# Four transformer blocks on one core: each norm joined to the stage before it, and one stage in place of load, first modulation and first norm

## What is computed

```python
def modulate(x, shift, scale):
    return layer_norm(x) * (1.0 + scale[:, None, :]) + shift[:, None, :]
```

## Time and profile before

| what | before |
|---|---|
| median of 3 runs | 3742.06 us (3732.88 to 3747.66) |
| the profiled execution's own time | 3748.66 us |
| its span, first to last instruction | 3746.9 us |
| mean granted TensorE clock | 0.957 |
| PE busy | 3398.1 us (91%) |
| DVE busy | 2617.8 us (70%) |
| ACT busy | 1756.9 us (47%) |
| DMA | 637.35 MB, mean 170 GB/s |

### The profile page before, as it was taken

How to read it: one execution, slowest core, us unless ns; L and a number is a source line. 1 busy time by engine, 2 the same in 40 slices (tenths; PEclk the granted TensorE clock), 3 DMA queues, 4 the chain that set the end, 5 groups by cost and what they waited for, 6 DMA issues and landing times. The chain is left out here.

```text
span 3746.9 us, 60692 instructions
## 1 busy us (share of the span) xinstructions
PE 3398.1 (91%) x19830; PEld 2989.5 (80%) x19830; DVE 2617.8 (70%) x5085; ACT 1756.9 (47%) x3251; POOL 224.5 (6%) x106
## 2 busy tenths in 40 slices
PE   4989889899999979989799999999968799898798
PEld 3877777789999968878587799999957699687697
DVE  5578669778787875566589687878756466445565
ACT  2353316755555544434239555555533254444353
POOL 0011000001011100100000011101101000001000
PEclk9989999999999989989899999999989899999899
DMA  5327432277777756237231577777741243552243
GB/s 208 122 65 268 164 119 91 92 236 249 256 246 242 250 180 195 64 128 254 79 124 40 189 243 242 249 254 247 241 162 71 79 167 137 173 187 96 91 186 118
DMA packets 256319, 637.35 MB, mean 170 GB/s; under 512 B 39088, under 2 KB 66224, under 8 KB 250000
## 3 DMA queue, kind: packets, MB, share of 16 engines
q1 hardware_dynamic: 217924, 561.56, 45.1%
q10 hardware_dynamic: 38220, 73.55, 5.7%
HBM read 633.89 MB, written 1.15 MB: 169 GB/s over the span
## 5 line engine op out<-in xcount | busy, mean ns | idle before, releaser
L147 PE MATMUL experts_ps_h<-uP_hi,experts_u_hi 128*128 128x256 f32 x1728 | 489.2, 283 | 1.6 <-DVE experts_u_lo L142 1.3
L149 PE MATMUL experts_ps_h<-uP_hi,experts_u_lo 128*128 128x256 f32 x1728 | 489.0, 283 | 0.0
L148 PE MATMUL experts_ps_h<-uP_lo,experts_u_hi 128*128 128x256 f32 x1728 | 488.9, 283 | 0.0
L142 DVE TENSOR_TENSOR experts_u_lo<-kept,experts_u_hi 128x512 fp32r<-128x512 f32 x432 | 354.2, 836 | 147.4 <-ACT experts_u_hi L139 135.6
L139 ACT ACTIVATE experts_u_hi<-kept 128x512 fp32r<-128x512 f32 x432 | 268.6, 630 | 342.3 <-PE experts_ps_h L149 271.1
L142 DVE TENSOR_TENSOR experts_v_lo<-u_w,experts_v_hi 128x512 fp32r<-128x512 f32 x432 | 298.2, 690 | 85.1 <-ACT experts_v_hi L139 77.5
L147 PEld LDWEIGHTS experts_ps_h<-uP_hi,experts_u_hi 128*128 128x128 f32 x1728 | 330.7, 191 | 15.0 <-DVE experts_u_lo L142 6.7
L147 PE MATMUL expert_y<-experts_v_hi,experts_w_hi 128*128 128x512 f32 x864 | 339.1, 392 | 1.1 <-DVE experts_w_lo L142 1.1
L148 PE MATMUL expert_y<-experts_v_lo,experts_w_hi 128*128 128x512 f32 x864 | 338.8, 392 | 0.0
L148 PEld LDWEIGHTS experts_ps_h<-uP_lo,experts_u_hi 128*128 128x128 f32 x1728 | 330.7, 191 | 7.5
L149 PE MATMUL expert_y<-experts_v_hi,experts_w_lo 128*128 128x512 f32 x864 | 336.1, 389 | 0.0
(11 more groups left out here) (547 smaller groups left out, 8105.9 us busy)
## 6 DMA issues: line engine op xcount, KB each, us to landing
u_w<-in_peer_v SPq DMA_DIRECT2D x256, 512.0 KB, 4.4
kept<-in_peer_u SPq DMA_DIRECT2D x216, 512.0 KB, 4.5
kept<-in_ada_w_all ACTq DMA_DIRECT2D x140, 512.0 KB
up_w<-in_ffn_w_up SPq DMA_DIRECT2D x44, 1024.0 KB, 5.5
od_in_w<-in_od_w_in SPq DMA_DIRECT2D x36, 1024.0 KB, 5.1
in_w<-in_w_in SPq DMA_DIRECT2D x48, 752.0 KB, 4.3
turns<-in_w_gate SPq DMA_DIRECT2D x32, 1024.0 KB, 6.4
down_w<-in_ffn_w_down SPq DMA_DIRECT2D x44, 512.0 KB, 3.3
```

The lines of the kernel that those rows point to most:

```text
L142: return dve.tensor_tensor(self.lo[at], value, self.hi[at].bitcast(F32), ALU.subtract)
L147: pe.matmul(out, left.hi[left_at], right.hi[right_at], start=start, stop=False, skip_group_check=skip)
L148: pe.matmul(out, left.hi[left_at], right.lo[right_at], start=False, stop=False, skip_group_check=skip)
L149: return pe.matmul(out, left.lo[left_at], right.hi[right_at], start=False, stop=stop, skip_group_check=skip)
```

## The change

The three first stages become one, `first_norm`. ada_w's columns come in eight transfers of 1 MB, in turn a quarter of the shift columns (512 columns, half of the rows; `wide`) and a quarter of the scale columns (256 columns, 1 KB runs; `slim`). DVE makes the shift half as before, PE the scale half directly: 64 f32 matmuls whose moving operand is one silu column and whose output is a column of scale; no row goes through DRAM. x's statistics and norm run between these. `norm_turn` is taken apart into the class `TurnedNorm`, whose steps are called from the stage before: `turn_project_norm`, `residual_norm_turn` and, for the norm after the first feed-forward, `conv_ffn` itself. Steps go row tile by row tile: ACT makes u of b = 0, DVE that of b = 1 in two halves; PE turns each tile on its own, and DVE and ACT take four chunks of 128 tokens each. Gate and residual are done in halves of 512 columns, as soon as that half of the projection is done; norm, g and b of `Residual` take two passes in place of three. The next stage's weights are issued in the joined stage, with one exception: of the expert choice only the first query weight (0.5 MB) is, while `choose_and_gate` itself now loads the keys (1 MB) and the other three. The third block's feed-forward tiles also hold the first weights of the fourth block's projection, which are loaded once the last of them is split. The seven norm stages that are joined and two of the three first ones end no more with the waits and the clearing of L76 to L78; a joined stage has the semaphores of both of its parts to clear.

```diff
+    def turn(self, pe, b, after_columns=True):
+        if after_columns:
+            pe.wait_ge(self.cols_done, 1)
+        for h in range(2):
+            pe.wait_ge(self.u_done[b], h + 1 if b else 1)
+            for k in range(h * 4, h * 4 + 4):
+                mm = pe.transpose(self.ps[:, b, k], self.u[:, b, k * P:(k + 1) * P], self.g.ident[:])
+            mm.then_inc(self.turned, 1)
...
+    def first_rows(self, act):
+        act.wait_ge(self.rstd_done, 1)
+        act.activation(self.u[:, 0], self.x[:, 0], ACT.Identity, bias=0.0 if self.rms else self.minus[:],
+                       scale=self.rstd[:, 0]).then_inc(self.u_done[0], 1)
...
+    def second_rows(self, dve, link):
+        dve.wait_ge(self.root_done, 2)
+        link(dve.reciprocal(self.rstd[:, 1], self.sd[:, 1]))
+        for h in range(2):
+            at = slice(h * 512, (h + 1) * 512)
...
+            else:
+                ins = dve.tensor_scalar(self.u[:, 1, at], self.x[:, 1, at], self.mv[:, 1, 0:1], self.rstd[:, 1],
+                                        ALU.subtract, ALU.mult)
+            ins.then_inc(self.u_done[1], 1)
...
+    def half_on_vector(self, dve, b):
+        dve.wait_ge(self.turned, 2 * b + 1)
+        for k in range(0, 4):
+            ins = dve.tensor_scalar(self.uT[:, k, b * P:(b + 1) * P], self.ps[:, b, k], self.scale[:, k:k + 1], self.cols[:, k:k + 1],
+                                    ALU.mult, ALU.add)
+        ins.then_inc(self.uT_vector, 1)
+
+    def half_on_act(self, act, b):
+        act.wait_ge(self.turned, 2 * b + 2)
+        act.wait_ge(self.cols_done, 1)
+        for k in range(4, KD):
+            ins = act.activation(self.uT[:, k, b * P:(b + 1) * P], self.ps[:, b, k], ACT.Identity, bias=self.cols[:, k:k + 1],
+                                 scale=self.scale[:, k:k + 1])
+        ins.then_inc(self.uT_act, 1)
+
...
+    def high(self, act, b):
+        for h, done in enumerate((self.uT_vector, self.uT_act)):
+            act.wait_ge(done, b + 1)
+            at = (slice(None), slice(h * 4, h * 4 + 4), slice(b * P, (b + 1) * P))
+            self.uP.write_hi(act, at, self.uT[at]).then_inc(self.hi_done, 1)
...
+def first_norm(nc, name, g, consts, c_all, x_in, ada_w, ada_b, x, uP, memory, ahead):
+    WIDE, SLIM, HK = 512, 256, KD // 2
+    SLIMS = D // SLIM
...
+                def load_wide(j):
+                    v, h = divmod(j, 2)
+                    at = slice(h * HK, (h + 1) * HK)
+                    sync.dma_start(wide[v][:, at], w[:, at, v * WIDE:(v + 1) * WIDE]).then_inc(wide_in[j], 16)
+
+                sync.dma_start(c16[:, 0], c_all[0]).then_inc(c_in, 16)
+                sync.dma_start(c16[:, 1], c_all[2]).then_inc(c_in, 16)
+                for j in range(SLIMS):
+                    load_wide(j)
+                    sync.dma_start(slim[j], w[:, :, D + j * SLIM:D + (j + 1) * SLIM]).then_inc(slim_in[j], 16)
                 for first in ahead:
                     first(sync)
+                sync.dma_start(g.iota[:], consts[1]).then_inc(iota_in, 16)
+                sync.wait_ge(iota_in, 16)
...
+                def slim_products(j):
+                    pe.wait_ge(slim_in[j], 16)
+                    for c in range(SLIM // P):
+                        at = KD + j * (SLIM // P) + c
+                        for k in range(KD):
+                            mm = pe.matmul(ps_c[:, at:at + 1], slim[j][:, k, c * P:(c + 1) * P], g.silu[:, 0, k:k + 1],
+                                           start=k == 0, stop=k == KD - 1)
+                    return mm
+
+                def wide_sums(v):
+                    pe.wait_ge(acc_done, v + 1)
+                    for c in range(WIDE // P):
+                        at = v * (WIDE // P) + c
+                        mm = pe.matmul(ps_c[:, at:at + 1], acc[:, v, c * P:(c + 1) * P], ones[:], start=True, stop=True)
...
+                slim_products(0)
+                slim_products(1)
+                norm.turn(pe, 0, False)
+                wide_sums(0)
+                slim_products(2)
+                norm.turn(pe, 1, False)
+                slim_products(3)
+                wide_sums(1).then_inc(sums_done, 1)
+                stay_awake(pe, ps_w[:, 0:T], g.ident[:], x[:, 0, 0:T], 7)
...
+                act.dma_start(g.ident[:], consts[0]).then_inc(ident_in, 16)
+                act.dma_start(bias[:], ada_b[0:2 * D].rearrange("(k p) -> k p", p=P)).then_inc(bias_in, 16)
+                act.dma_start(x[:], x_in).then_inc(x_in_done, 16)
...
+                add_up(0)
+                dve.wait_ge(x_in_done, 16)
+                norm.stats(dve, link, 0)
+                add_up(1)
+                norm.stats(dve, link, 1)
+                norm.first_factors(dve, link)
+                add_up(2)
+                norm.second_rows(dve, link)
+                add_up(3)
+                dve.wait_ge(bias_turned, 1)
+                dve.wait_ge(sums_done, 1)
+                link(dve.tensor_copy(norm.cols[:], ps_c[:, 2 * KD:4 * KD]))
+                link(dve.tensor_tensor(norm.cols[:], norm.cols[:], ps_c[:, 0:2 * KD], ALU.add))
+                link(dve.tensor_scalar_add(norm.scale[:], norm.cols[:, KD:2 * KD], 1.0))
...
+    def weigh(self, dve, link, b, h):
+        at = slice(h * 512, (h + 1) * 512)
+        r = self.r[:, b, at]
         dve.wait_ge(self.gate_in, 16)
...
-            link(dve.reciprocal(self.sd[:, b], self.sd[:, b]))
-            link(dve.tensor_scalar(x[:, b], self.r[:, b], self.mv[:, b, 0:1], self.sd[:, b], ALU.subtract, ALU.mult))
-            link(dve.tensor_tensor(x[:, b], x[:, b], self.g[:], ALU.mult))
-            link(dve.tensor_tensor(x[:, b], x[:, b], self.b[:], ALU.add))
+        link(dve.tensor_tensor(r, self.y[:, b, at], self.gate[:, at], ALU.mult))
+        link(dve.scalar_tensor_tensor(out=r, in0=self.x[:, b, at], scalar=DN_ALPHA, in1=r, op0=ALU.mult, op1=ALU.add))
+        link(dve.bn_stats(self.st[:, b, h, :], r))
+
+    def close(self, dve, link, b):
+        link(dve.bn_aggr(self.mv[:, b, :], self.st[:, b].rearrange("p a b -> p (a b)")))
+        dve.tensor_scalar_add(self.sd[:, b], self.mv[:, b, 1:2], LN_EPS).then_inc(self.stats_done, 1)
+
+    def centre(self, dve, link, b):
+        dve.wait_ge(self.rows_in, 32)
+        link(dve.scalar_tensor_tensor(out=self.r[:, b], in0=self.r[:, b], scalar=self.mv[:, b, 0:1], in1=self.g[:],
+                                      op0=ALU.subtract, op1=ALU.mult))
+
+    def finish(self, dve, link, b):
+        dve.wait_ge(self.root_done, b + 1)
+        link(dve.reciprocal(self.sd[:, b], self.sd[:, b]))
+        link(dve.scalar_tensor_tensor(out=self.x[:, b], in0=self.r[:, b], scalar=self.sd[:, b], in1=self.b[:],
+                                      op0=ALU.mult, op1=ALU.add))
...
+def turn_project_norm(nc, name, g, src, pre, x, gate_row, ln_rows, row, gain_cols, uP, uT, ahead, room=None, spare=None):
...
+                norm.load(sync)
+                for first in ahead:
+                    first(sync)
...
+                    if b:
+                        norm.turn_rows(pe)
...
+                        if h:
+                            mm.then_inc(y_done, 1)
+                for b in range(TB):
+                    norm.turn(pe, b)
+                stay_awake(pe, y[:, 0, 0:T], g.ident[:], x[:, 0, 0:T], 7)
...
+                if ln_rows:
+                    res.root(act, 0)
+                norm.root(act, 0)
+                norm.first_rows(act)
+                if ln_rows:
+                    res.root(act, 1)
+                norm.half_on_act(act, 0)
+                norm.root(act, 1)
+                norm.high(act, 0)
+                norm.half_on_act(act, 1)
+                norm.high(act, 1)
...
+                for h in range(2):
+                    weigh(0, h)
+                if ln_rows:
+                    res.close(dve, link, 0)
+                    res.centre(dve, link, 0)
+                    res.finish(dve, link, 0)
+                norm.stats(dve, link, 0)
+                norm.columns(dve, link)
+                norm.first_factors(dve, link)
+                for h in range(2):
+                    weigh(1, h)
+                if ln_rows:
+                    res.close(dve, link, 1)
+                    res.centre(dve, link, 1)
+                    res.finish(dve, link, 1)
+                norm.stats(dve, link, 1)
+                norm.half_on_vector(dve, 0)
+                norm.second_rows(dve, link)
+                norm.low(dve, 0)
+                norm.half_on_vector(dve, 1)
+                norm.low(dve, 1)
...
+                pre.load(sync, 1, 1, pre.sources)
+                keys.first(sync)
+                for n in range(2, RING):
+                    pre.load(sync, n, n, pre.sources)
...
+def residual_norm_turn(nc, name, g, x, y, gate_row, ln_rows, row, gain_cols, uP, uT, ahead):
...
+                for b in range(TB):
+                    for h in range(2):
+                        res.weigh(dve, link, b, h)
+                    res.close(dve, link, b)
```

(27 more changed lines are left out.)

## The result

The changed kernel takes 3709.78 us in the median of four runs (3696.51 to 3715.1), the kernel before, with its new runs, 3744.86 us (3732.88 to 3749.33): a ratio of 0.9907, 95% interval 0.9889 to 0.9924, so 28 to 42 us less. The forecast was 3695 in a range of 3668 to 3711: the direction was right and the range held, if only by 1.2 us at its upper end, but 47.2 us were forecast and 35.1 measured. The profiled execution has a span of 3705.4 us against 3746.9, which is 41.5.

A forecast was written before the change was run, and what follows sets the result against it. TensorE is busy nearly everywhere, so gains come only where it waits: 37.4 us at the joins plus 9.8 at the first stage, 47.2 off the median 3742.06, gives 3695; range 3668 to 3711.

The forecast's parts named there:

- The start: First stage, up to the first product: start at 55.7 us in place of 65.47, a gain of 9.8 us.
- the low clock: TensorE in the first stage stays at clock .50: a slim part takes 7.0 us, first product at 55.7.
- the other level: First rival: clock rises during the slim products, 3.7 us a part, first product at 42.9, total 3682; chance .33.
- weight loads as the pace: In the first stage's slim products, 32 weight loads set a part's time: 7.0 us or 3.7 by clock.
- The joins: Norms joined to the stages before: 14.2 + 8.0 + 13.6 + 2.4 − .8 = 37.4 us gained.
- Before the choice: Two gaps from last product to expert choice: 17.5 us for 25.1; with .5 off for keys, 2 × 7.1 = 14.2 gained.
- the four 128-column chunks: Chunks of a row tile in the joined norms: 1.1 us, estimated between bounds of 1.1 and 2.2.
- the matmuls without use: stay_awake, seven f32 matmuls ending each joined norm: 4.13 us before the expert choice, 3.3 at the last output projections.
- the last projections: Output projections of the last two blocks: gap of 12.0 us for 18.8, 2 × 6.8 = 13.6 gained.
- after the first feed-forward: Gap behind the first feed-forward: 20.2 us for 22.6, with 38 semaphores to clear; 2.4 gained.
- after the experts: Two gaps behind the experts, second taken like the first: 29.0 us for 33.0, 2 × 4.0 = 8.0 gained.
- Rival 2: Joins give back 16 us: colder stay_awake, 1.3 at each of seven, and next stages starting slow; total 3712; chance .15.

## Why the prediction was right and where it was not

**The start** went by its steps: the low clock chosen against the other level, weight loads as the pace, 7.0 us a part, 55.7 for 56.76. Of the 1.1 us that it came late, .6 are in the chunks, split and remainder behind the sums (6.5 us from the first copy of the columns where I had 5.9) and the rest ahead of them. The Trainium skill (TensorE: Matmul & The Clock Gate, Part 1: The HAM clock gate) has a gate that activity releases; the trace of the changed kernel doesn't show it released by these products, for TensorE stood nowhere between 13.1 and 47.0 us and the last part took as long as the first.

**The joins** had the right mechanism, and nearly every term a size that was too small in the kernel after. Before the choice I had 17.5 us, measured 18.8. Two kinds of terms were mis-sized. One is the price of small pieces: the four 128-column chunks are 1.36 us on VectorE where I took 1.1, the lower end of my own bounds, and u's half was done at 9.2 and not 8.8. The other is larger, .75 of the 1.3 us: the matmuls without use took 4.88 and not 4.13. They started with the clock still low (.50 from 468 to 472), after TensorE had stood for 8.5 us; where it was kept busy in that gap they took 3.19. Over the seven joins they took 4.88, 4.15, 4.58, 5.02, 3.77, 5.13 and 3.68 us, where I had 4.13 or about 4, and 3.3 at the last projections. The stage's end was 2.8 for 2.7.

At the last projections it is 12.9 of 12.0, here by the pieces, since VectorE ends within .2 us of TensorE; after the first feed-forward 21.8 of 20.2, mostly the 5.13; after the experts 29.6 of 29.0 (1377.04 to 1406.60). The second place after the experts I had taken like the first, but what follows there is an RMS norm, with shorter statistics: before, it took 31.8 us (2749.47 to 2781.28) and not 33.0, so with the very 29.0 of the forecast after (2718.00 to 2747.00) it gained 2.8 and not 4.0. All this is 5.7 us of the 12.1 that were missing: 31.7 in the gaps, 37.4 forecast. The start's 1.1 comes on top, and the rest is the difference between profiles and medians.

**Rival 2** is the one that came nearest by its number (3712), and its first half is in the gaps: colder matmuls at the joins' ends, .75 us before the choice where it had 1.3, and 3 to 4 us in all, an estimate from the seven durations above and from which engine ended last. Its price was read too high: the .65 is that of 486 to 488 us, while over the whole of the seven matmuls, 485.49 to 489.62, the clock was .77. Its sum has slips as well: 1.3 and half of 1.3 at seven joins are 13.7 us and not 16, and 3695 with 16 and 2 is 3713. The range's upper end, 3711, is 3695 with the 16; with 13.7 it would have been 3709 and the measured 3709.78 outside. That the range held is luck. Its second half, a next stage that starts low, is there in three places: behind the start (.50 from 57 to 61 us, where before it was 1.00 from the first product on; 1.2 us more), behind the first feed-forward (.50 from 3168 to 3173), and in the last feed-forward, after which the products start cold.

```profile
3493.00:3495.00 2.00, 1.66 (x12) 1.48 (x12) 0.73 (x2) 1.83 (x2) 0.00 (x0) 0.95 0.26 39
3495.00:3501.00 6.00, 5.29 (x25) 5.32 (x26) 1.69 (x2) 0.17 (x1) 0.00 (x0) 0.50 0.76 257
3501.00:3504.00 3.00, 3.00 (x24) 3.00 (x24) 2.20 (x4) 1.33 (x2) 0.00 (x0) 0.90 0.03 8
```

From 3495 to 3501 the clock is .50, in before it was back at 1.00 4 us after the stage's start, and the products behind are 2.3 us later, the very last ones 3.3; with the eight half passes this feed-forward is 212.1 us long where it was 207.5. In three other places it went the other way: the second choice, the delta stage and the first feed-forward began at .50 before (1850 to 1852, 2782 to 2784, 2993 to 2996) and at 1.00 after (1820 to 1824, 2747 to 2751, 2950 to 2954).

**What remains open** is the difference between 40 us of gaps and 35 of medians, which is within the interval. The profiles of 14 kernels give a reason why single pairs can't settle it: the second attention stage, the same instructions in all of them, takes 100.3 to 111.1 us, and goes roughly by its mean granted clock. Twelve of them lie between 100.3 and 104.3; the kernel before and the one with the matmuls ahead are the two at 110 and 111. Before, after, with the matmuls ahead, with 64 columns:

```profile
1542.00:1652.00 110.00, 92.39 (x624) 79.86 (x624) 72.17 (x193) 51.22 (x161) 16.07 (x16) 0.84 0.19 55
```

```profile
1528.00:1631.00 103.00, 84.06 (x625) 73.48 (x624) 71.67 (x194) 51.49 (x162) 15.93 (x16) 0.92 0.21 59
```

```profile
1526.00:1637.00 111.00, 92.36 (x624) 80.01 (x624) 72.08 (x193) 51.18 (x161) 15.85 (x16) 0.84 0.19 55
```

```profile
1531.00:1632.00 101.00, 82.77 (x625) 72.45 (x626) 71.33 (x194) 51.43 (x162) 16.00 (x16) 0.95 0.21 60
```

In the pair before and after, 7 us of this stage are with the change, and elsewhere other stages take as much back. These 7 us are not the change's doing: the kernel before with clears of ranges has 103.2 us here, at .92, and the one with the old first stages 103.0. What decides the clock of a stage of short bursts was not tried; that an earlier edit shifts it is not shown.

Keys and query weights, moved into the choice, cost no more than was put on them: the stage is 219.38 us long where it was 218.92, and 218.99 where it was 220.19. They were not preloaded again in a run of their own.

## What to carry to other kernels

Joining stages pays by the waits between the steps, so count the steps that stay and price each in the shape that it will have: halves and quarters of a tile cost more than their share (four chunks of 128 columns 1.36 us where four of 256 took 1.90), and the error adds up over the joins. Matmuls that only bridge a wait must be priced at the clock that the wait leaves. Before moving work between stages, look at what the end of one costs: there, clearing semaphores by ranges took 33 us out of the ends, and 36 to 41 out of the time, with no step of the computation moved. And where TensorE is fed one column at a time, let the weights be the moving operand: here a part took 3.62 us in place of 6.95.

## What the hardware did that was not expected

One-column products, issued without a gap from 13.1 to 26.9 us, left the clock low: 32 weight loads took 6.95 us in the last part as in the first. A clock that had been raised ahead of them fell during the first part (4.65 us, then 6.99), though with waits of 1.16 and 1.05 us around that part. With 64 columns it was the same (7.07); with 256 columns and weights of one column the clock rose and a part took 3.62. Clearing a semaphore costs GpSimd .07 us per instruction, and a range costs as one. A shorter stage end also left the clock up in the stage behind it (1.00 in place of .50, 2.6 us). A stage of unchanged instructions took between 100.3 and 111.1 us with a granted clock between .95 and .84, which is more than the whole start was worth.
